# Moving four modulation products per layer into the first attention tile, and splitting the load of the output weights

## What is computed

```python
for l in range(2):
    mod = silu(c) @ w_mod[l] + b_mod[l]         # 6 * 1024 values; also for c_ctx
    sh1, sc1, g1, sh2, sc2, g2 = split(mod, 6)  # the same six for the context
    h = rms_norm(x, norm_mix[l]) * (1 + sc1) + sh1
    u = split_cols(h @ w_in[l])                 # 2400 columns, four head groups
    a, b, c_, d = gqa(u), neighbourhood(u), differential(u), latent(u)
    x = x + g1 * (concat(a, b, c_, d) @ w_out[l])
    h2 = rms_norm(x, norm_ffn[l]) * (1 + sc2) + sh2
    x = x + g2 * moe_ffn(h2, ...)               # 16 experts, top 2, one shared expert
return rms_norm(x, final_norm)
```

## Time and profile before

| what | before |
|---|---|
| median of the runs | 1645.83 us (3 runs, 1645.29 to 1653.87) |
| the profiled execution: time | 1647.25 us |
| its span in the trace | 1645.1 us |
| mean granted clock of TensorE | 0.989 of full speed |
| projection units and rounds of layer 0 / layer 1 | about 35 to 250 us / 921 to 1114 us |
| first attention tile of layer 0 / layer 1 | 250 to 325 us / 1114 to 1183 us |
| further attention tiles of layer 0 / layer 1 | 326 to 590 us / 1183 to 1379 us |
| experts' stage of layer 0 / layer 1 | 592 to 916 us / 1379 to 1645 us |

### The profile page before, as it was taken

One profiled execution on the slowest core, in us unless ns is written; L12 is line 12 of the kernel. 1 busy time (PEld: TensorE's weight loads), 2 busy tenths in 40 slices (PEclk: granted clock), 3 DMA queues, 4 the chain that ended last, 5 costly groups with the idle time before them and its releaser, 6 DMA issues.

```text
span 1645.1 us, 26409 instructions
## 1 busy us (share of the span) xinstructions
PE 1572.1 (96%) x10090; PEld 1054.5 (64%) x10090; DVE 837.5 (51%) x1791; ACT 428.8 (26%) x922; POOL 196.8 (12%) x348
## 2 busy tenths in 40 slices
PE   6999999899999989999999999999899999999996
PEld 4655445666665567788888555555666666688873
DVE  2222534567665657555555721434667665644345
ACT  1322113455454410000000312113455541000001
POOL 0110102000000000222221110202000000021212
PEclk9999999999999999999999999999999999999998
DMA  9764230600001286689888774331501016478885
GB/s 354 235 236 154 103 45 7 202 1 32 22 26 39 94 300 255 211 319 335 329 323 305 260 257 154 130 65 36 178 1 40 14 61 224 182 277 315 311 319 193
DMA packets 113425, 285.60 MB, mean 174 GB/s; under 512 B 32945, under 2 KB 42863, under 8 KB 103535
## 3 DMA queue, kind: packets, MB, share of 16 engines
q1 hardware_dynamic: 101942, 263.13, 46.1%
q0 software_dynamic: 10800, 20.99, 3.4%
q10 hardware_dynamic: 584, 0.14, 0.0%
HBM read 265.47 MB, written 40.37 MB: 186 GB/s over the span
## 4 chain that ended last, share of the span: by engine, by line
PE 82%; DMA 6%; SPq 5%; DVE 3%; issue 2%; ACT 1%; POOL 0%; POOLq 0%; DVEq 0%; ACTq 0%
PE S L1577 15%; PE S L1238 14%; PE S L1317 7%; PE B L1382 7%; PE S L1588 7%; PE B L1365 6%; PE PT L1334 5%; PE B L1257 3%; PE B L1144 2%; PE PT L1512 2%; DMA arena<-in_w_mod 2%; PE S L1257 2%; PE S L1448 1%; DMA arena<-in_moe_w_up 1%; PE PT L1472 1%
## 5 line engine op out<-in xcount | busy, mean ns | idle before, releaser
L1238 PE MATMUL S<-arena 128*128 128x512 f32 (+3 forms) x768 | 300.2, 541 | 3.8 <-ACT arena L903 3.8
L1577 PEld LDWEIGHTS S<-arena 128*128 128x128 f32 x2304 | 263.6, 192 | 19.4 <-issue 19.3
L1577 PE MATMUL S<-arena 128*128 128x128 f32 x2304 | 265.3, 275 | 1.4 <-DMA arena<-in_moe_w_up 0.9
L1238 PEld LDWEIGHTS S<-arena 128*128 128x128 f32 x768 | 141.8, 193 | 125.4 <-issue 105.2
L1009 ACT ACTIVATE arena<-S,nmax 128x768 f32<-128x768 f32 (+1 forms) x200 | 161.9, 813 | 163.8 <-DVE nmax L2062 120.6
L2062 DVE TENSOR_REDUCE nmax<-S 128x1 f32<-128x768 f32 (+1 forms) x168 | 133.1, 825 | 75.7 <-PE S L1317 65.6
L1382 PE MATMUL B<-arena 128*128 128x512 f32 x320 | 156.5, 613 | 1.9 <-DVE arena L2116 1.9
L1334 PEld LDWEIGHTS PT<-cst,arena 128*128 128x128 f32 x832 | 94.6, 141 | 84.6 <-issue 57.4
L1317 PE MATMUL S<-arena 64*128 64x256 f32 (+5 forms) x624 | 144.7, 504 | 4.1 <-ACT arena L1009 2.4
L1334 PE MATMUL PT<-cst,arena 128*128 128x128 f32 x832 | 121.4, 278 | 19.0 <-issue 11.3
L1588 PE MATMUL S<-arena 128*128 128x512 f32 x288 | 129.6, 593 | 1.2 <-DVE arena L2195 1.2
(11 more groups left out here) (321 smaller groups left out, 1775.1 us busy)
## 6 DMA issues: line engine op xcount, KB each, us to landing
arena<-in_w_mod SPq DMA_DIRECT2D x24, 2048.0 KB, 11.3
arena<-in_moe_w_gate SPq DMA_DIRECT2D x36, 1024.0 KB, 6.4
arena<-in_moe_w_up SPq DMA_DIRECT2D x36, 1024.0 KB, 9.5
arena<-in_moe_w_down SPq DMA_DIRECT2D x36, 1024.0 KB, 6.8
arena<-in_w_in SPq DMA_DIRECT2D x6, 2048.0 KB, 11.5
arena<-y SPq DMA_DIRECT2D x20, 512.0 KB, 5.9
arena<-mod SPq DMA_DIRECT2D x16, 512.0 KB, 16.6
arena<-in_tokens SPq DMA_DIRECT2D x12, 512.0 KB, 10.3
```

Source lines behind the costliest of these rows:

```text
L1238: mm = pe.matmul(ubank[u % 4][:, c0:PANEL_W[p]], hT[:, k, t * P:(t + 1) * P], panel[p][:, k, c0:], start=k == 0, stop=k == KT - 1)
L1577: mm = pe.matmul(to, wgu[b][:, w, k * DE + h * P:k * DE + (h + 1) * P], XT[b][:, k, :], start=k == 0, stop=k == KT - 1)
```

## The change

Chunks 4 to 7 stay in the projection, at other units. Chunks 8 to 11 are multiplied in steps 4, 6, 7 and 9 of the first attention tile (FAR_STEPS) and kept in a free half of the buffer OT. Their weights are loaded after the bias tables, chunk 10 into the array `hT` once the last neighbourhood unit has read it, chunk 11 into slot 2. The output weights are loaded in two parts, rows 0 to 3 before chunk 11 and rows 4 to 7 when all twelve chunks are multiplied. `far_store` then writes the four chunks to DRAM, and only after that come the `vec` loads and, in the unchanged lines behind them, the eight copies. PE calls `values` ahead of `product(.., 0)`. Neighbourhood units 6 and 7 go together into step 5 and share a bank. Layer 1 begins with 13 idle products (`idle_products`). The first two row tiles of the experts' stage are loaded ahead of the shared weights. In the experts' stage some turns of the hidden rows, `s_down(2)`, `s_out` and the routing steps change places. In the final sums some additions change places, `c_late` waits for each half of a tile by itself, and the last tile is scaled and stored in two halves.

```diff
-NB_IN_STEP = {0: [2], 1: [3], 2: [4], 3: [5], 4: [6], 5: [7]}
+NB_IN_STEP = {0: [2], 1: [3], 2: [4], 3: [5], 5: [6, 7]}
-MODS_AT = {3: 4, 5: 5, 7: 6, 9: 7, 11: 8, 13: 9, 15: 10, 17: 11}
+MODS_AT = {3: 4, 6: 5, 9: 6, 12: 7}
+FAR = 8
+FAR_STEPS = {4: 8, 6: 9, 7: 10, 9: 11}
-PIECES = {..., 6: (8, 11), 7: (11, 14), 9: (14, 16)}
+PIECES = {..., 6: (8, 10), 7: (10, 12), 8: (12, 14), 9: (14, 16)}
+        far_row, far_norm = OT[1][:, 0:4, :], OT[1][:, 4:6, :]
-        mod_w = [[slot[0], slot[2], mod_w2, mod_w3] + [slot[2]] * (NMCH - 4),
-                 mod_late + [slot[1], mod_w5, slot[2], mod_w5, slot[2], mod_w5] + [slot[2]] * (NMCH - 9)]
+        mod_w = [[slot[0], slot[2], mod_w2, mod_w3] + [slot[2]] * 6 + [mod_w2, slot[2]],
+                 mod_late + [slot[1], mod_w5, slot[2], mod_w5] + [slot[2]] * 3 + [mod_w2, slot[2]]]
...
                 def mod_store(l):
+                    sp.wait_ge(s["mod_row"], NMCH * l + FAR)
+                    for r in range(2):
+                        sp.dma_start(mod_d[l][r, 2 * D:4 * D].rearrange("(n q c) -> q n c", q=4, c=MODQ),
+                                     mod_row0[r:P:32, 4:FAR]).then_inc(s["mod_stored"], 16)
+                    sp.wait_ge(s["mod_stored"], 64 * l + 32)
+
+                def far_store(l):
+                    sp.wait_ge(s["mod_row"], NMCH * (l + 1))
                     sp.wait_ge(s["mod_gain"], 2 * l + 2)
                     for r in range(2):
-                        sp.dma_start(mod_d[l][r, 2 * D:6 * D].rearrange("(n q c) -> q n c", q=4, c=MODQ),
-                                     mod_row0[r:P:32, 4:NMCH]).then_inc(s["mod_stored"], 16)
-                    sp.wait_ge(s["mod_stored"], 32 * (l + 1))
+                        sp.dma_start(mod_d[l][r, 4 * D:6 * D].rearrange("(n q c) -> q n c", q=4, c=MODQ),
+                                     far_row[r:P:32]).then_inc(s["mod_stored"], 16)
+                    sp.wait_ge(s["mod_stored"], 64 * (l + 1))
...
+                mod_load(l, 9, 9)
                 sp.wait_ge(s["u_mm"], UNIT0[l + 1])
+                mod_load(l, 10, 0)
                 for kv in range(2):
                     src = A["w_out"][l][P * kv:P * kv + P, :].rearrange("(b p) n -> p b n", p=64)
                     sp.dma_start(wout[64 * kv:64 * kv + 64, 0:2, :], src).then_inc(s["wout_in"], 16)
-                sp.dma_start(wout[:, 2:KT, :], A["w_out"][l][2 * P:D, :].rearrange("(k p) n -> p k n", p=P)).then_inc(s["wout_in"], 16)
+                sp.dma_start(wout[:, 2:4, :], A["w_out"][l][2 * P:4 * P, :].rearrange("(k p) n -> p k n", p=P)).then_inc(s["wout_in"], 16)
+                mod_load(l, 11, 10)
+                sp.wait_ge(s["mod_mm"], NMCH * (l + 1))
+                sp.dma_start(wout[:, 4:KT, :], A["w_out"][l][4 * P:D, :].rearrange("(k p) n -> p k n", p=P)).then_inc(wout_late_in, 16)
+                far_store(l)
                 for stream in range(2):
                     for n, w in enumerate((2, 4, 3)):
                         sp.dma_start(vec[:, 3 * stream + n, :], mod_d[l][stream, w * D:(w + 1) * D].partition_broadcast(P)).then_inc(s["vec_in"], 16)
...
                     sp.wait_ge(s["scored"], 2 * NS * gend)
+                    for b in range(2):
+                        hs_load(b)
...
                 def s_first_loads():
-                    for b in range(2):
-                        hs_load(b)
                     sp.wait_ge(s["pv_done"], NJ * gend)
...
+                    if l and u == 0:
+                        idle_products(7)
...
+                if l:
+                    idle_products(6)
                 transpose_x(0)
...
                         pe.wait_ge(s["wout_in"], 48 * (l + 1))
+                        pe.wait_ge(s["mod_row"], NMCH * (l + 1))
...
                     tp, kp = divmod(n - 1, NS)
+                    job = job_at(l, n)
+                    if job:
+                        values(*job)
                     after = 1 <= n <= NS * nt
                     if after and STEPS[kp][0] != "d":
                         product(tp, kp, 0)
-                    job = job_at(l, n)
-                    if job:
-                        values(*job)
                     for piece in pieces:
                         out_piece(t - 1, piece)
+                    if n in FAR_STEPS:
+                        pe.wait_ge(s["u_evac"], min(UNIT0[l] + NTU + 6, UNIT0[l + 1]) if n < 5 else UNIT0[l + 1])
+                        pe.wait_ge(s["mod_row"], NMCH * l + FAR_STEPS[n])
+                        mod_product(l, FAR_STEPS[n], B7)
                     if after:
                         product(tp, kp, 1)
...
                         if t == 0:
                             route_counts()
+                            s_turn_hid(1)
                             pe.wait_ge(s["r_took"], 1)
                             mod_product(1, 1, B6)
...
                     s_up(3)
+                    s_down(2)
                     pe.wait_ge(s["r_took"], 2)
                     route_table()
-                    pe.wait_ge(s["s_hts"], g(2) + 1)
                     s_turn_hid(3)
-                    s_down(2)
                     s_down(3)
...
+                    if n in FAR_STEPS:
+                        mod_row(l, FAR_STEPS[n], B7[:, :])
+                        if FAR_STEPS[n] == NMCH - 1:
+                            mod_gain(l, 1)
...
-                    dve.scalar_tensor_tensor(x3[t], x3[t], h2s[:, 2 + b:3 + b], fgain, ALU.mult, ALU.mult).then_inc(s["c_x3"], 1)
+                    for c0, c1 in [(0, D)] if t < TL - 1 else [(0, 512), (512, D)]:
+                        dve.scalar_tensor_tensor(x3[t][:, c0:c1], x3[t][:, c0:c1], h2s[:, 2 + b:3 + b], fgain[:, c0:c1], ALU.mult, ALU.mult).then_inc(s["c_x3"], 1)
```

More of the change, by code:

```diff
@@ L274, in program @@
         tmpA, tmpB = take(512), take(512)
+        XT_START = take.at[0]
         xt = [take(D) for _ in range(2)]
@@ L325, in program @@
         PTa, PTb, PTd = take(NTOK), take(NTOK + 2 * P), [take(NTOK), take(NTOK + P)]
+        OT_START = take.at[0]
         OT = [take(KT, P) for _ in range(2)]
+        assert OT_START + KT * P >= XT_START and OT_START + 2 * KT * P <= XT_START + 2 * D
+        far_row, far_norm = OT[1][:, 0:4, :], OT[1][:, 4:6, :]
         dO, dSq = take(P), take(P)
@@ L863, in _ @@
                 for t in range(nt):
-                    sp.wait_ge(s["c_x3"], gc(t) + 1)
-                    sp.dma_start(dst(span(t * P, P)), x3[t]).then_inc(s[f"c_stored{t % 2}"], 16)
+                    parts = [(0, 512), (512, D)] if l and t == nt - 1 else [(0, D)]
+                    for n, (c0, c1) in enumerate(parts):
+                        sp.wait_ge(s["c_x3"], gc(t) + 1 + n)
+                        sp.dma_start(dst(span(t * P, P))[:, c0:c1], x3[t][:, c0:c1]).then_inc(s[f"c_stored{t % 2}"], 16)
                 for b in range(2):
-                    sp.wait_ge(s[f"c_stored{b}"], 16 * (gend // 2))
+                    sp.wait_ge(s[f"c_stored{b}"], 16 * (gend // 2 + l * b))
         @block.scalar
@@ L1874, in mod_row @@
                     dve.wait_ge(s["mod_mm"], n + 1 + NMCH * l)
[L1875 removed]
+                    row = far_row[:, n - FAR, :] if n >= FAR else mod_rows_at(l, n)[:, n, :]
                     dve.tensor_tensor(row, bank[:, 0:MODQ], row, ALU.add).then_inc(s["mod_row"], 1)
@@ L1881, in mod_gain @@
                     dve.wait_ge(s["mod_row"], n + 2 + NMCH * l)
-                    a = mod_rows_at(l, n)[:, n:n + 2, :]
-                    dve.scalar_tensor_tensor(a, a, 1.0, mod_norm_at(l, half), ALU.add, ALU.mult).then_inc(s["mod_gain"], 1)
+                    a = far_row[:, 0:2, :] if half else mod_rows_at(l, n)[:, n:n + 2, :]
+                    dve.scalar_tensor_tensor(a, a, 1.0, far_norm if half else mod_norm_at(l, half), ALU.add, ALU.mult).then_inc(s["mod_gain"], 1)
                 def modcol_of(l, bank):
@@ L2416, in _ @@
                     route_slots()
+                    s_out(0)
                     route_blocks_hot()
@@ L2447, in e_out, with e_block @@
                                              ALU.mult, ALU.mult).then_inc(s["e_y"], 1)
-                def e_block(blk, u, b, more, first, out_first, meanwhile=None):
+                def e_block(blk, u, b, more, first, out_first):
                     last = not first or b
```

94 lines of the change are left out of this document (48 added, 46 removed).

## The result

The changed kernel takes 1686.41 us (median of 4 runs, 1682.22 to 1692.03), the kernel before 1646.3 us beside it: ratio 1.0232, 95% interval 1.0203 to 1.0261. The forecast was 1666 us, 1.2% slower, with a range to 1678. The direction was right, the time is 8 us beyond the range. The span went from 1645.1 to 1682.4 us.

The account below looks back on a forecast made before the run. The prediction took PE, busy 96% of the span, as the bound. From 1645.1 us it took 30.3 for projection and seams, added 46.2 for held copies and 4.4 for half clock: 1665.4 of span, 1666 us predicted, range 1646 to 1678.

Parts of the forecast that it names:

- The copies are held: Start of tile 1, both layers: copies queue on SP behind stores and `vec`; 46.2 us lost, plus 4.4 at half clock.
- E: End of the last chunk in each layer's first attention tile, forecast at 326.0 and 1184.7 us.
- The first tile takes the chunks nearly free: First attention tile: holes take most of the four added products; ready at 327.0 and 1185.7 instead of 325.1 and 1183.3.
- The projection's 17.6: Projection, both layers: eight modulation products leave, 15.1 us, and three waits for `w_mod` go, 2.5 us.
- Sum 12.7: Edits at the seams: layer 1's start 3.2, row loads 5.2, routing 1.0, steady tiles 2.3, tail 1.0 us saved.
- 5.2 us for the row loads: Start of the experts: loading first row tiles early saves 4.1 us in layer 0 and about 1.1 in layer 1.
- The idle products: Start of layer 1: thirteen idle products fill two holes at no cost and keep the clock up, 2.7 us saved.
- The tail's 1.0: End of the kernel: the last scaling of 1.28 us is stored in halves, 1.0 us saved, bounds 0 and 3.
- The steady tiles' 2.3 and the routing's 1.0: Steady attention tiles: a moved piece and earlier `values` save 2.3 us; layer 0's routing: counts ahead of `s_out` save 1.0.
- Rival 1: Start of tile 1: the copies are not held and the gains stand alone, 1619 us; chance 0.08.
- Rival 2: Start of tile 1: copies held for less, wait 4.9 us shorter per layer, gains up to 7 larger, 1649 us; chance 0.16.
- Rivals 3 and 4: Projection doesn't give its 15.1 us, 1676, chance 0.12; chunks' loads late in both layers' first tile, 1676, chance 0.06.

Follow-up runs that it names:

- experiment 14: Changed kernel with the eight copies issued early, without the early row loads and the edits of the tail: 1630.16 us, ratio 0.9882 to the kernel before.
- experiment 4: Chunk move with the copies issued early and none of the five edits at the seams: 1636.42 us, ratio 0.9911 to the kernel before.
- experiment 1: Changed kernel with the eight copies issued right behind chunk 11's load, ahead of the wait for all twelve products: 1634.81 us, ratio 0.9895 to the kernel before.

## Why the prediction was right in kind and wrong in size

- **The copies are held: right.** The chain has the forecast's links, the last copy is issued at E + 16.0 as written, and early copies take the whole wait away. The size was 4.9 us short: the last copy landed at E + 24.8 where 22.4 was forecast, and the waits were 47.7 us instead of 42.8. The term that was mis-sized is the data behind the stores. At 401 GB/s `vec` should have been through at E + 17.0 and the copies 5.4 us later; the trace has 249 GB/s at the start of `vec` and 202 near the end.
- **The first tile takes the chunks nearly free: right.** From the first score to PE ready, the kernel with chunks only takes 76.7 us in layer 0 and 71.0 in layer 1, before 74.7 and 68.7. Forecast: 1.9 and 2.4 more; found: 2.0 and 2.3. In the changed kernel it is 3.3 and 3.4; chunk 9 waits 1.35 and chunk 10 1.25 us for their loads in layer 1 (forecast 1.7 for chunk 9 and nothing for chunk 10). The closeness is partly luck, as the second profile of the kernel before has 73.0 and 68.2, so 3.7 and 2.8 more against it. The forecast counted 1.4 us for a score at half clock behind the hole of 2.01. In the second profile the same hole is there, and the same score runs at full clock:

```profile
305.81 1.56 PE L1317 MATMUL S<-arena 64*128 64x512 f32 x8
```

- **The projection's 17.6: right.** The first score of layer 0 comes 8 to 11 us earlier than in the shown profile in all kernels with the move, for 10.1 forecast (four chunks and the 2.5 of waits). In layer 1 the kernel with chunks only gains 9.1 us from the first unit to the first score against the shown profile and 7.7 against the second one, for 7.6 forecast.
- **The failed step is the seams' "Sum 12.7".** Alone they give a ratio of 1.0016 instead of 0.992. With the 4.9 us of the waits these are 17.6 us, and the measured ratio is 18 us above the forecast one (20 by the medians). I read five holes, and took each as saved once its releaser was moved, without asking what the move delays. The largest, 5.2 us for the row loads, turned into a loss (1.0017): four terms stand in the earlier trace rows, but the queue past which the loads were moved has the store on which the last output products depend. The idle products were taken to cost nothing, but they take 2.78 and 3.21 us in holes of 2.04 and 1.66, and of the 2.7 some 0.5 was left. The tail's 1.0 was nothing. The steady tiles' 2.3 and the routing's 1.0 lie inside their intervals, and so does no gain at all.
- **What stays open.** The five edits one by one have ratios whose deviations from 1 add to -0.0003 (rows +17, routing -6, steady tiles -7, idle products -9, tail +2, in units of 0.0001), together they have +0.0016, and on the chunk move they come to +0.0036 (1.0232 less 1.0196), on the move with early copies to -0.0016 (0.9895 less 0.9911). With intervals of 0.2 to 0.3% these are one result, near nothing, but it isn't shown where between 6 us lost and 4 us gained it lies. The routing, the steady tiles and the idle products alone add to -0.0022, or 3.6 us of the 6.0 forecast, and experiment 14, which has these three on the kernel of experiment 4, is 0.0029 below that; each is within its interval. Nor is it shown what made up for waits 6.7 us longer in the chunk move's 32.3.
- **Rivals.** Rival 1 (copies not held, 1619) fell, yet its second condition, copies ahead of the stores, is experiment 1, at 1634.8 (ratio 0.9895, or 1629 in the terms of the forecast): the 1619 counted the seams. Rival 2 needed a chain below 12.3 us; even with the stores landing after 1.72 us it was 23.0. Rivals 3 and 4 fell: the projection gave its gain, and the waits for the chunks' loads in the first tiles are 3.0 us in all (0.37 in layer 0, 2.6 in layer 1).

## What to carry to other kernels

When a producer is moved later, follow the issuing queue behind it to the first transfer that someone waits for: here eight unrelated copies stood behind one late wait, and issuing them ahead of it turned a loss of 2.3% into a gain of a little over 1%. A hole in a timeline is saved only if the edit that closes it delays nothing else; price what the moved transfers push back, make a filler shorter than its hole, and count small holes at well under their length: here the three harmless edits had 6.0 us forecast, and their runs add to 3.6, not told from nothing. Read a phase that hangs on weight loads, or a clock behind a hole of 2 us, from two profiles before an effect of the change is seen in it.

## What the runs showed that I had not expected

- A store of a few kilobytes lands 6.45 us after its issue behind a 2 MB load on its queue, and 1.72 us after it without, in the same kernel.
- The same program waited 0.9 and 7.7 us for expert weights in two profiled executions, and 29 of its runs spread over 15 us. With half of these weights 6 runs spread over 5 us, but with the seams 9 runs over 9, so that the weights make the spread isn't shown.
- The issue of one load of shared weights occupied SP for 2.05 us, and for 5.04 us with two row loads more in front of it (3.85 in the changed kernel), so that a store behind it was issued late, and then also took 7.70 us to land instead of 6.13.
- Behind the same hole of 2.01 us in the same program the granted clock was down in one execution (a score of 2.90 us) and not in another (1.56 us).
